# Both attentions of a two-layer encoder step: a new order of each head pair's work on four engines

## The reference

```python
def _trunk(x, pos, past, p):
    for layer in range(DEPTH):                                   # 2
        h = h + 0.5 * _swiglu(_rms_norm(h, g), w_in, w_out)      # D_FF = 2816
        hn = _rms_norm(h, p['g_mix'][layer])
        if layer < N_A:                                          # MLA, chunk-causal
            q, lat, kpe = _mla_project(hn, ...)                  # q = rms_norm(concat(nope, rope))
            k, v = _mla_keys(lat_all, kpe_all, ...)              # 16 heads, 96 wide; values 64
            o = _attention(q, k, v, pos, k_pos, True)
        else:                                                    # FoX, causal, forget bias
            q = _rms_norm((hn @ w_b_q).reshape(b, l, 16, 64), g)
            o = _attention(q, k_all, v_all, pos, k_pos, False, c_q, c_k)
        h = h + o.reshape(b, l, -1) @ w_out
        h = h + 0.5 * _swiglu(_rms_norm(h, g2), w_in2, w_out2)
        if layer == N_A - 1:
            fox = _fox_shared(h, ...)
# _attention: softmax(q k^T / sqrt(d) [+ c_q - c_k] + mask) v, the queries in blocks of 128
```

## Time and profile before

| | before |
|---|---|
| median of 3 runs | 2445.28 us (2443.11 to 2445.39) |
| the profiled execution, its own time | 2441.57 us |
| its span, first to last instruction | 2439.8 us |
| MLA attention, first score tile to first product of the output projection | 473.85 to 776.00 us |
| FoX attention, end of the query projection to first product of the output projection | 1771.80 to 1994.45 us |
| mean granted TensorE clock, share of full | 0.960 |

### The profile page before, as it was taken

One profiled execution on the slowest core, in us unless ns is written; L12 is line 12 of the kernel. 1 busy time (PEld: TensorE's weight loads), 2 busy tenths in 40 slices (PEclk: granted clock), 3 DMA queues, 4 the chain that ended last, 5 costly groups with the idle time before them and its releaser, 6 DMA issues. The chain is left out here.

```text
span 2439.8 us, 45128 instructions
## 1 busy us (share of the span) xinstructions
PE 2264.4 (93%) x16514; PEld 2175.0 (89%) x16514; DVE 1716.3 (70%) x2708; ACT 1075.8 (44%) x1801; POOL 320.5 (13%) x281
## 2 busy tenths in 40 slices
PE   4999999888897899999999999999978888999997
PEld 4999999878787899999977999999767778999997
DVE  8976974566665897598445984985466648975973
ACT  5532543455554553254324551553245645532531
POOL 1000001143432100000122000001143321000001
PEclk9999999889889999999999999999978889999998
DMA  2222232100001222223123222222212112222221
GB/s 108 99 94 93 95 113 70 38 19 10 19 1 44 80 101 106 78 102 105 65 86 106 105 105 94 87 104 82 82 28 48 42 40 85 95 104 84 96 105 60
DMA packets 72810, 187.55 MB, mean 77 GB/s; under 512 B 40720, under 2 KB 42288, under 8 KB 61440
## 3 DMA queue, kind: packets, MB, share of 16 engines
q1 hardware_dynamic: 71424, 181.67, 22.0%
q0 software_dynamic: 1280, 4.49, 0.5%
HBM read 178.79 MB, written 7.35 MB: 76 GB/s over the span
## 5 line engine op out<-in xcount | busy, mean ns | idle before, releaser
L585 PE MATMUL ps<-xs_hi,w_hi 128*128 128x272 f32 x1408 | 410.1, 291 | 50.9 <-DVE w_lo_more L1639 28.4
L587 PE MATMUL ps<-xs_hi,w_lo 128*128 128x272 f32 x1408 | 407.9, 290 | 0.0
L586 PE MATMUL ps<-xs_lo,w_hi 128*128 128x272 f32 x1408 | 407.0, 289 | 0.0
L1105 ACT ACTIVATE w_hi<-raw 128x1408 fp32r<-128x1408 f32 (+4 forms) x123 | 145.4, 1187 | 500.5 <-PE ps L610 244.9
L1134 ACT ACTIVATE w_hi<-w_blocks 128x1024 fp32r<-128x1024 f32 x176 | 186.8, 1061 | 322.5 <-PE ps L587 156.0
L585 PEld LDWEIGHTS ps<-xs_hi,w_hi 128*128 128x128 f32 x1408 | 266.4, 189 | 54.6 <-issue 29.6
L585 PE MATMUL ps<-xs_hi,w_hi_more 128*128 128x272 f32 x1056 | 306.0, 290 | 2.4 <-ACT scratch L1180 1.8
L586 PE MATMUL ps<-xs_lo,w_hi_more 128*128 128x272 f32 x1056 | 305.3, 289 | 0.0
L610 PE MATMUL ps<-hid_hi,w_hi 128*128 128x272 f32 x1312 | 272.8, 289 | 9.1 <-DVE w_lo L1609 5.4
L610 PE MATMUL ps<-hid_hi,w_lo 128*128 128x272 f32 x1312 | 271.4, 288 | 0.0
L610 PE MATMUL ps<-hid_lo,w_hi 128*128 128x272 f32 x1312 | 271.4, 288 | 0.0
(11 more groups left out here) (266 smaller groups left out, 5143.9 us busy)
## 6 DMA issues: line engine op xcount, KB each, us to landing
w_blocks<-w_ffn_in SPq DMA_DIRECT2D x88, 1024.0 KB, 4.8
raw<-w_ffn_out SPq DMA_DIRECT2D x64, 704.0 KB, 4.1
raw<-w_b_kv SPq DMA_DIRECT2D x16, 512.0 KB, 3.2
raw<-w_a_out SPq DMA_DIRECT2D x8, 512.0 KB, 3.2
raw<-w_b_q SPq DMA_DIRECT2D x8, 512.0 KB, 3.3
raw<-w_b_out SPq DMA_DIRECT2D x8, 512.0 KB, 3.3
raw<-w_a_in SPq DMA_DIRECT2D x4, 672.0 KB, 4.1
raw<-w_a_qup SPq DMA_DIRECT2D x8, 288.0 KB, 2.8
```

The lines of the kernel that those rows point to most:

```text
L585: pe.matmul(out, lhs[0], rhs[0], start=start, stop=False, skip_group_check=more)
L586: pe.matmul(out, lhs[0], rhs[1], start=False, stop=False, skip_group_check=more)
L587: return pe.matmul(out, lhs[1], rhs[0], start=False, stop=stop, skip_group_check=more)
L1105: act.activation(wh[par][:, 0:n], raw[par][:, 0:n], ACT.Copy).then_inc(w_hi, 1)
```

## The change

The same instructions are issued; their order in each pair changes on all four engines, and with it the banks and the waits. `first_head` and `second_head` give way to one function for a pair: `pair_a` in the MLA, `pair_b` in the FoX.
- PE, MLA: s10, t00, s11, t01, t02, s12, s13, t03, staging q0 and q1, s14, values of head 0 for tiles 0 to 2, staging p0, p1, c0, the last value tile, c1, then a third of `project_q`, the stream's rows, the rest of `project_q`, two of the five groups of `project_kv`, and the other three groups dealt out among t10 to t13 and the score tiles of the next pair.
- PE, FoX: the values of head 0 are made in three pieces between staged tiles, those of head 1 in two, with s03, t13 and s04 between them.
- ACT, DVE and POOL: their operations stand in matching order. `stage_values` stands in the FoX after `exp` of the third tile, in the MLA still before it. `norm_keys` stands ahead of the staging. The squares of the queries, the extraction of the last key groups and the splitting of the projection's next weights are dealt out among the tiles. On POOL, `queries` still stands ahead of `normalise` of head 0.
- The loops: four pairs of the MLA still run in the hardware loop (now pairs 1 to 4); in the FoX seven pairs on PE and six on the others run in one loop, where before they were written out as in the MLA.
- `FIRST_BANKS` now names the bank of every tile of the opening, `first_uses` follows from it.

```diff
--- before.py
+++ after.py
...
 ATT = {
-    "pe": sum([[f"t0{j}", f"s1{j}"] for j in range(4)], []) + ["s14", "pv0"] + [f"t1{j}" for j in range(4)] + ["pv1"],
-    "act": skewed([f"pt0{j}" for j in range(4)], [f"exp1{u}" for u in range(5)]) + [f"pt1{j}" for j in range(4)],
-    "dve": ["m10", "pt00", "m11", "pt01", "r10", "m12", "pt02", "r11", "m13", "ps0", "pt03", "r12", "m14", "r13", "r14", "d14"]
-    + ["pt10", "pt11", "pt12", "ps1", "pt13"],
+    "pe": ["s10", "t00", "s11", "t01", "t02", "s12", "s13", "t03", "s14", "pv0", "t10", "t11", "t12", "t13", "pv1"],
+    "act": ["pt00", "pt01", "exp10", "pt02", "exp11", "exp12", "pt03", "exp13", "exp14", "pt10", "pt11", "pt12", "pt13"],
+    "dve": ["m10", "m11", "pt00", "m12", "pt01", "r10", "pt02", "m13", "ps0", "pt03", "r11", "r12", "m14", "r13", "r14",
+            "d14", "pt10", "pt11", "pt12", "ps1", "pt13"],
     "pool": [f"d1{u}" for u in range(4)],
+}
+ATTX = ATT | {
+    "pe": ["s10", "t00", "t01", "s11", "t02", "s12", "s13", "t03", "s14", "pv0", "t10", "t11", "t12", "t13", "pv1"],
+    "dve": ["m10", "m11", "m12", "r10", "pt00", "r11", "pt01", "m13", "pt02", "r12", "ps0", "pt03", "m14", "r13", "r14",
+            "d14", "pt10", "pt11", "pt12", "ps1", "pt13"],
...
-                every += [(f"kv{n}", p + 2, projects, [("projk", "act", f"v{n}")]) for n in range(5)]
-            every += turned(1)
+                every += staged("q0", "q1", "p0", "p1", "c0", "c1") + queries(0) + staged("s") + queries(1, 2) + keys(0, 1)
+                every += turned("10", "11") + keys(2, 3) + turned("12", "13") + keys(4)
+            else:
+                every += staged("q0", "p0", "p1", "c0", "q1", "c1", "s") + turned("10", "11", "12", "13")
...
-                    if hh == 0:
+                def values(hh, p, tiles=range(4), ahead_of_last=None):
+
+                    if hh == 0 and tiles[0] == 0:
                         pe.wait_ge(*L["stagev"]["pool"].at("v", p))
 
                         pe.wait_ge(*L["out"]["dve"].at("o", p - 1))
-                    pe.wait_ge(*att["dve"].at(f"pt{hh}3", p))
+                    pe.wait_ge(*att["dve"].at(f"pt{hh}{tiles[-1]}", p))
...
+                def pair_a(p, stages, projects):
+                    uses, before = w_uses(L, p, True, stages, projects, mla), w_uses(L, p - 1, True, True, stages, mla)
+                    scores(1, 0, p)
+                    turn(0, 0, p, uses, before)
+                    scores(1, 1, p)
+                    turn(0, 1, p, uses, before)
+                    turn(0, 2, p, uses, before)
+                    scores(1, 2, p)
+                    scores(1, 3, p)
+                    turn(0, 3, p, uses, before)
+                    if stages:
+                        staged("q0", p + 1, uses, before)
+                        staged("q1", p + 1, uses, before)
                     scores(1, 4, p)
-                    else:
+                    values(0, p, range(3))
+                    if stages:
+                        staged("p0", p + 1, uses, before)
+                        staged("p1", p + 1, uses, before)
+                        staged("c0", p + 1, uses, before)
+                    values(0, p, range(3, 4))
+                    if stages:
+                        staged("c1", p + 1, uses, before)
+                    if projects:
+                        project_q(p + 2, uses, before, range(1), lambda: bank_of("ts", uses, before))
+                    if stages:
+                        staged_samples(p + 1, uses, None if projects else before)
+                    if projects:
+                        project_q(p + 2, uses, before, range(1, 3))
+                        project_kv(p + 2, uses, before, range(2))
                     for j in range(4):
                         turn(1, j, p, uses, before)
+                        if projects and j == 3:
+                            project_kv(p + 2, uses, before, range(4, 5))
+                        if stages and j < 2:
                             scores(0, j, p + 1)
+                        if projects and j == 1:
+                            project_kv(p + 2, uses, before, range(2, 3))
+                        if stages and j == 1:
+                            scores(0, 2, p + 1)
+                        if projects and j == 1:
+                            project_kv(p + 2, uses, before, range(3, 4))
+                        if stages and j > 1:
+                            scores(0, j + 1, p + 1)
+                    values(1, p)
+
+                def pair_b(p, stages):
+                    uses, before = w_uses(L, p, True, stages, False, mla), w_uses(L, p - 1, True, True, stages, mla)
+                    scores(1, 0, p)
+                    turn(0, 0, p, uses, before)
+                    turn(0, 1, p, uses, before)
+                    scores(1, 1, p)
+                    turn(0, 2, p, uses, before)
+                    scores(1, 2, p)
+                    scores(1, 3, p)
+                    turn(0, 3, p, uses, before)
+                    if stages:
+                        staged("q0", p + 1, uses, before)
+                    scores(1, 4, p)
+                    if stages:
+                        staged("p0", p + 1, uses, before)
+                        staged("p1", p + 1, uses, before)
+                        staged("c0", p + 1, uses, before)
+                    values(0, p, range(1))
+                    if stages:
+                        staged("q1", p + 1, uses, before)
+                        staged("c1", p + 1, uses, before)
+                    values(0, p, range(1, 2), (lambda: bank_of("ts", uses, before)) if stages else None)
+                    if stages:
+                        staged_samples(p + 1, uses)
+                    values(0, p, range(2, 4))
+                    turn(1, 0, p, uses, before)
+                    turn(1, 1, p, uses, before)
+                    if stages:
+                        scores(0, 0, p + 1)
+                    turn(1, 2, p, uses, before)
+                    if stages:
+                        scores(0, 1, p + 1)
+                        scores(0, 2, p + 1)
+                    values(1, p, range(1))
+                    if stages:
+                        scores(0, 3, p + 1)
+                    turn(1, 3, p, uses, before)
                     if stages:
                         scores(0, 4, p + 1)
+                    values(1, p, range(1, 4))
...
+                    if not first:
+                        stage_values(p, odd)
+                    exp(1, 2, p)
+                    if stages:
+                        stage_part("q0", p + 1)
                     split_p(0, 3, p)
-                    for u in range(2, 5):
-                        exp(1, u, p)
...
+                    exp(1, 1, p)
+                    exp(1, 2, p)
+                    stage_values(p)
+                    split_p(0, 3, p)
...
+                def pair_a(p, first, stages, projects, splits):
+                    top(1, 0, p)
+                    top(1, 1, p)
+                    split_p(0, 0, p)
+                    top(1, 2, p)
+                    split_p(0, 1, p)
+                    inverse_sum(1, 0, p)
+                    split_p(0, 2, p)
+                    if not first:
+                        heads_out(p - 1)
+                        if stages:
+                            norm_keys(p + 1)
+                    top(1, 3, p)
+                    split_p(0, 3, p)
+                    if stages:
+                        stage_part("q0", p + 1)
+                        stage_part("q1", p + 1)
+                        if first:
+                            norm_keys(p + 1)
+                        for name in ("p0", "p1", "c0", "c1"):
+                            stage_part(name, p + 1)
+                    if projects:
+                        take_q(p + 2, range(1))
+                    inverse_sum(1, 1, p)
+                    inverse_sum(1, 2, p)
                     top(1, 4, p)
...
+                def pair_a(p, odd, first, stages, projects):
+                    if first:
+                        power_keys(1)
+                    else:
+                        stage_values(p, odd)
+                    if stages:
                         shared_keys(p + 1)
                     normalise(1, p)
-
-                def second_head(p, stages, projects):
-                    if mla and projects:
+                    if projects:
                         queries(p + 2)
                     if stages:
                         normalise(0, p + 1)
-                    if mla and projects:
+                    if projects:
                         power_keys(p + 2)
```

More of the change, by code:

```diff
@@ L840, in project_kv, with staged @@
                         mm.then_inc(prk["pe"].sem if n < 4 else w_used, 1)
-                def turn_staged(it, uses, before, between=None):
-                    if mla:
-                        pe.wait_ge(*prq["pool"].at("qn", it))
-                    else:
```

(32 more changed lines are left out.)

486 lines of the change are left out of this document (264 added, 222 removed).

## The result

The median of four runs is 2369.73 us (2368.68 to 2371.25), beside 2445.34 us (2443.11 to 2446.86) for four runs of the kernel before: ratio 0.9692, 95% interval 0.9675 to 0.9709, 75.6 us less. The forecast was 2377.8 us in a range of 2358 to 2412. The profiled execution took 2368.68 us, its span is 2366.5 us, 73.3 us shorter than before.

The account below looks back on a forecast made before the run. TensorE, busy 93% of the span, was taken as the bound, with idle time and lost clock in the attentions recoverable. Gains of 67.5 us took 2441.6 to 2374.1; plus 3.7 for the median gave 2377.8 us, range 2358 to 2412.

Parts of the forecast that it names:

- The two waits: Both attentions: s14 behind `stage_values` (1.7 and 1.9 us); MLA key transposes behind `norm_keys` (1.1 us); new order covers both.
- The content at full clock: TensorE's work per steady pair, unchanged by the reordering: 29.7 us in the MLA, 18.2 us in the FoX.
- The MLA walk: Steady MLA pair followed list by list: s13 idles 0.4 us, s14 0.55; 0.95 in all, 1.5 taken.
- The FoX walk: Steady FoX pair followed list by list: five TensorE waits, at most 1.0 us each; 2.4 in all, 2.7 taken.
- The clock: Steady steps: clock loss falls from 3.9 to 0.8 us in the MLA, from 3.5 to 1.3 in the FoX.
- The last MLA pairs: Pair without projection becomes like a FoX pair with `norm_keys`, 22.5 us (-5.6); the last pair gains 1.0 us.
- The openings: Starts of both attentions: MLA opening with pair 0 -8.0 us, first FoX stretch, hanging on GpSimd's scaling, -2.5 us.
- outside: Stretches outside the two attentions: no gain or loss, staying within 1 us.
- A: Rival: GpSimd's loop sets the MLA step at 35 us, about 2393 us in all; chance 0.10.
- B: Rival: the clock does not come back; losses of 3.9 and 3.5 us a step stay, about 2411 us; chance 0.12.
- C: Rival: no gain, TensorE's waits in the attentions only change their names, 2441 to 2445 us; chance 0.04.
- D: Rival: slower, VectorE and GpSimd block each other in both attentions, MLA steps 41.5 us, about 2461 us; chance 0.06.

Follow-up runs that it names:

- fox_values_early: Changed kernel with ScalarE's FoX values copy moved back ahead of exponential 2 of head 1: 2365.3 us, ratio 0.9668.
- mla_hold: Changed kernel with ScalarE's two values copies issued twice in every MLA pair from pair 1, ahead of exponential 2 of head 1: 2375.3 us, ratio 0.9712.
- fox_hold1: Changed kernel with FoX values copied ahead of exponential 2 of head 1 and both copies issued once more in front: 2382.0 us, ratio 0.9730.
- fox_hold2: As fox_hold1, with 1.4 us more of ScalarE's copies in front: 2393.4 us, ratio 0.9778.
- fox_v0_block: Changed kernel with FoX values of head 0 in one block, the stream's rows' bank asked for ahead of c1: 2433.8 us, ratio 0.9957.
- tail_full: Changed kernel with the last two MLA pairs in their own order: values dealt out, inverse sums and exponentials ahead of staging: 2364.5 us, ratio 0.9673.
- fox_old: Changed kernel with the FoX functions of before put back on all four engines: 2397.4 us, ratio 0.9809.
- ends: tail_full plus both openings reordered: FoX GpSimd power and scaling behind pairs 0 and 1, MLA key squares behind first maxima: 2353.2 us, ratio 0.9625.

## Why the prediction was right, and where it was not

*The two waits.* Right: s14 waits in neither attention (0.55 us were forecast for the MLA), and the key transposes no longer wait for `norm_keys`. But the reason given for the FoX (the exponential ahead of the copy) is not needed: `fox_values_early`. And the expectation of `mla_hold` put the 0.3 us that are left at s14; they are s13's, and s14 started from 0.

*The content at full clock.* 29.7 and 18.2 us were taken; PE is busy for 29.85 and 18.80 at a clock of 1.00. The FoX term was 0.6 short.

*Idle time.* The MLA walk gave 0.95 and I kept 1.5; it was 0.8, s13's 0.3 (0.4 in the walk) and p0's 0.4 to 0.6. The walk has no wait at p0; its bank, that of t03, was not looked at. The FoX walk gave 2.4 and I took 2.7; it was 1.1. The walk's 1.0 us for the bank of the stream's rows was 0.6, and t03's 0.45 came out at 0.4; s13, p1 and the last values did not wait. The estimates of pieces by columns were good to some tenths, and summed to an error of 1.3 us, 1.6 with what was added on top.

*The clock: the term that was mis-sized.* I took 0.8 and 1.3 us a step, a share of the old loss in line with the holes left. It was 0 in both in the profiled run of after. The runs show the loss to come in lumps, and not in each pass: with holes of 0.3 to 0.6 us none in after, but 1.7 us in one FoX step of six in five other kernels with the same FoX order; with one hole of 0.8 to 1.0 us sometimes (`mla_hold`, `fox_hold1`), with 1.9 in each step (`fox_hold2`), and most where three waits follow each other in the transposes (`fox_v0_block`). What decides whether a pass has its lump, no run shows. With content, idle time and clock the FoX step was 18.2 + 2.7 + 1.3 = 22.2 in the forecast, 18.8 + 1.1 + 0 = 19.9 on the chip: 13.8 us over six steps. For the MLA 1.36 x 5 = 6.8 us. The rule of the Trainium skill ("TensorE: Matmul & The Clock Gate", Part 4) by which transposes would not count as activity did not hold the FoX down: with 44 transposes a pair its steps ran at 1.00. Whether transposes weigh less once there are holes, no run here separates.

*The last MLA pairs: the step that failed.* "Now like a FoX pair", 22.5 us, was not worked out on the four lists. The MLA order has six staged parts on VectorE ahead of three inverse sums, which a projection covers in the steady pairs and nothing covers in pair 6. The forecast gave -6.6 us for the two pairs, the chip +3.7; `tail_full` takes 7.7 of these 10.3 us back, and with it pair 6 is 23.0 us long. Some 3 us of the 10.3 are the long fall of the clock in pair 6, which `fox_old` did not have with the same code.

*The openings.* -10.5 forecast, -8.8 measured. The MLA's -6.9 is in part luck: the same code took 57.1 to 58.3 us in seven other kernels and 54.4 and 54.5 in two, against 54.5 in after. The FoX one hung on GpSimd's scaling as the prediction said, and on the power of 6.75 us ahead of it, which the prediction did not name; `ends` shows that this was open to an order.

*The errors cancelled in part.* -20.6 us in the steady steps, +13.1 at the ends, +1.7 outside (forecast: within 1): span -73.3 against -67.5. The median of after then lies 1.05 us above its profiled run, where 3.7 had been added for before's. The forecast is 8.1 us off, and nearer than its terms by luck.

*The rivals.* A did not come, but was nearer than its argument had it: 1.28 us more of GpSimd cost 3.1 us in most steps, at the values, not in the loop. B did not come, and `fox_hold2` shows that one hole of 1.9 us a pair would have brought its FoX part. (Its sum takes 1.1 us of idle for the MLA where the forecast takes 1.5; with 1.5 it would be 2 us higher.) C and D did not come. D's sign did: an operation of GpSimd of twice its length in each steady MLA pair, as below. Its price did not: the 0.4 to 0.6 us ahead of p0 at most, an estimate, since `norm_keys` is 0.7 us longer in after than alone and p0's bank hangs on it.

## What to carry over

Price a hole in TensorE's work twice: by its length, and by the lump of clock that it may bring; taking out waits of some tenths of a microsecond can be worth more than their sum. Before a stretch's change is put down to an edit, look up the same stretch in the other kernels that have its code. An order of work tuned to a loop's steady pass should be walked once more, list by list, for the passes where its cover is missing, and the last of several inputs of a wait is the one to move. Ask of each thing that is deferred to "meanwhile" which later wait stands behind it on its queue.

## What was not expected of the hardware

VectorE's `norm_keys` (two operands in SBUF) took 2.07 to 2.26 us beside GpSimd's work, and 1.34 us alone in the MLA opening; GpSimd's scaling of the shared keys took 2.28 us beside it and 1.16 us alone, its subtraction 2.38 and 1.28. The Trainium skill, "SBUF — State Buffer", section "Who interferes with whom", says that a VectorE instruction with two SBUF inputs contends with a GpSimd instruction that reads SBUF; the durations here agree. They depend on who starts first. In after GpSimd's subtraction starts 0.4 us ahead of `norm_keys` and keeps its 1.28 us; in `mla_hold` `norm_keys` starts 0.7 us ahead of it and keeps 1.36 us, and the subtraction takes 1.73 to 1.80. Each time the one that started later is longer by nearly (0.1 us less than) the time that the two overlapped.

In pair 6 the same instructions in the same order, with the same wait of 2.87 us, ran at a clock of 0.76 to 0.93 from kernel to kernel, 3 us apart.
